# Attention units rebuilt around full 128 x 128 tiles, with masks added by TensorE, in a two-model fp32 layer kernel

## The reference, in short

```python
# FX (block one): 4 heads of 128
s = q @ k.T + (F_q - F_k);  s = where(k_pos <= q_pos, s, -inf);  p = softmax(s);  out = p @ v
# block two, 4 heads of 64, S = 512, per layer:
# MLA: heads of 96 = 64 + 32 rotary, values of 64, causal softmax
# NSA: o = g0 * attend(q, k_compressed (31 blocks)) + g1 * attend(q, selected) + g2 * attend(q, window)
#      (S = 512 makes selection and window causal over all keys; one key head for four query heads)
# DSA: score = sum_h w_h * relu(q_idx_h . k_idx), keep the top 128 keys of each query, softmax over them
# stick-breaking:
z = q @ k.T * scale;  mask = k_pos < q_pos
log_1m = where(mask, log_sigmoid(-z), 0);  after = cumsum(log_1m, reverse=True) - log_1m
a = where(mask, exp(log_sigmoid(z) + after), 0);  out = a @ v
```

## Time and profile before

| | |
|---|---|
| median of three runs | 3871.75 us |
| profiled execution, device time | 3873.97 us |
| its span, first to last instruction | 3872.2 us |
| mean granted TensorE clock | 0.898 |
| TensorE busy | 3588.0 us (93%) |
| VectorE, ScalarE, POOL busy | 1634.7, 1315.0, 335.9 us |

### The profile page before, as it was taken

How to read it: one execution, slowest core, us unless ns; L and a number is a source line. 1 busy time by engine, 2 the same in 40 slices (tenths; PEclk the granted TensorE clock), 3 DMA queues, 4 the chain that set the end, 5 groups by cost and what they waited for, 6 DMA issues and landing times. The chain is left out here.

```text
span 3872.2 us, 37493 instructions
## 1 busy us (share of the span) xinstructions
PE 3588.0 (93%) x14768; PEld 2731.7 (71%) x14768; DVE 1634.7 (42%) x2663; ACT 1315.0 (34%) x2225; POOL 335.9 (9%) x156
## 2 busy tenths in 40 slices
PE   6988889989999999898978999999998989699998
PEld 5755668878888888775545788878886655367886
DVE  3143431135343333356674533343344476654334
ACT  2324532233232222324354423232223243544222
POOL 0311324410000000130010000000002200100000
PEclk8988879999999999997556999999999965689999
DMA  3210213322333333320000233323332100012332
GB/s 125 77 38 26 77 40 97 98 82 95 96 98 98 98 95 97 101 71 28 1 1 22 87 96 95 98 87 94 96 98 95 55 17 1 0 55 87 96 96 76
DMA packets 76783, 279.82 MB, mean 72 GB/s; under 512 B 8768, under 2 KB 9024, under 8 KB 76224
## 3 DMA queue, kind: packets, MB, share of 16 engines
q1 hardware_dynamic: 76608, 277.42, 23.1%
HBM read 275.29 MB, written 2.10 MB: 72 GB/s over the span
## 5 line engine op out<-in xcount | busy, mean ns | idle before, releaser
L502 ACT ACTIVATE w_hi<-raw_slabs 128x1024 fp32r<-128x1024 f32 x496 | 524.3, 1058 | 1325.5 <-PE ps L542 1181.0
L517 DVE TENSOR_TENSOR w_lo<-raw_slabs,w_hi 128x1024 fp32r<-128x1024 f32 x376 | 459.9, 1224 | 740.3 <-ACT w_hi L502 740.1
L542 PE MATMUL ps<-in_hi,w_hi 128*128 128x512 f32 x1904 | 746.4, 392 | 9.9 <-DVE in_lo L816 9.9
L542 PE MATMUL ps<-in_hi,w_lo 128*128 128x512 f32 x1904 | 744.0, 391 | 0.0
L542 PE MATMUL ps<-in_lo,w_hi 128*128 128x512 f32 x1904 | 744.0, 391 | 0.0
L542 PE MATMUL ps<-parts,w_hi 128*128 128x512 f32 x2304 | 712.3, 390 | 7.7 <-PEq L378 7.7
L517 POOL TENSOR_TENSOR w_lo<-raw_slabs,w_hi 128x1024 fp32r<-128x1024 f32 x120 | 302.7, 2524 | 2429.9 <-ACT w_hi L502 2429.9
L542 PEld LDWEIGHTS ps<-parts,w_hi 128*128 128x128 f32 x2304 | 433.3, 188 | 100.0 <-issue 10.0
L542 PE MATMUL ps<-parts,w_lo 128*128 128x512 f32 x1152 | 448.9, 390 | 0.0
L542 PEld LDWEIGHTS ps<-in_hi,w_hi 128*128 128x128 f32 x1904 | 359.0, 189 | 91.3 <-DVE in_lo L816 8.9
L542 PEld LDWEIGHTS ps<-in_hi,w_lo 128*128 128x128 f32 x1904 | 359.4, 189 | 75.4
(11 more groups left out here) (258 smaller groups left out, 3640.9 us busy)
## 6 DMA issues: line engine op xcount, KB each, us to landing
raw_slabs<-weights SPq DMA_DIRECT2D x508, 512.0 KB, 3.6
big<-rope SPq DMA_DIRECT2D x2, 2304.0 KB, 10.1
x_resid<-xT SPq DMA_DIRECT2D x8, 256.0 KB, 4.5
outT<-x_resid SPq DMA_DIRECT2D x8, 256.0 KB, 2.0
const_cols<-consts SPq DMA_DIRECT2D x1, 1088.0 KB, 9.4
scratch<-brow SPq DMA_DIRECT2D x1, 768.0 KB, 10.6
vector_cols<-vec SPq DMA_DIRECT2D x2, 45.5 KB, 10.3
vector_cols<-vec SPq DMA_DIRECT2D x1, 69.0 KB, 3.0
```

The source lines that it names most:

```text
L502: self.nc.scalar.activation(self.w_hi[:, m % SPLIT, :], self.raw[:, n % RAW, :], ACT.Copy)\
L517: (self.nc.gpsimd if i is None else self.nc.vector).tensor_tensor(self.w_lo[:, m % SPLIT, :], self.raw[:, n % RAW, :], self.w_hi[:, m % SP ...
L542: mm = k.nc.tensor.matmul(out, lhsT, rhs, start=(c == 0 and m == 0), stop=(last and m == 2))
```

## The change

1. Scores and values use the whole array. In block two a head's query tile is used with all 128 rows; keys that two heads share are copied into an even and an odd tile, in which the other head's 64 rows are zero (`HalfKeys`, on POOL in the MLA up-projection and the index phase). Values are taken 128 columns wide (the neighbour's columns give rows of the result that are not stored).
2. The mask is one more matmul, identity times mask, into the score's bank: 128 columns for causal masks, 32 for the compressed unit, the whole width for DSA's selection. The compressed unit has a 32nd key, a floor, in place of the 0/1 multiply. Scales move to the query projections or into the exponential.
3. VectorE's maximum and ScalarE's exponential read PSUM; the score bank is free after the exponential.
4. Stick-breaking goes unit by unit, with one activation table; the exponent is completed in PSUM by a matmul; VectorE copies the transposed blocks.
5. `ahead` in `ResidNorm` goes by limits, after tiles 2, 4 and 6.

```diff
+def score(k, u, bank):
+    nc, w = k.nc, u.width
+    for j, (lhsT, rhs) in enumerate(u.scores):
+        nc.tensor.matmul(k.ps[:, bank, 0:w], lhsT, rhs, start=(j == 0), stop=False)
+    n = u.mask.shape[1]
+    return nc.tensor.matmul(k.ps[:, bank, w - n:w], k.c("ident"), u.mask, start=False, stop=True)
+def turn(k, u, p, bank):
+    for a, w in u.blocks:
+        mm = k.nc.tensor.transpose(k.ps[0:w, bank, a:a + P], p[:, a:a + w], k.c("ident"))
+    return mm
+def weigh(k, u, pt, bank):
+    for j, ((a, w), val) in enumerate(zip(u.blocks, u.values)):
+        mm = k.nc.tensor.matmul(k.ps[:, bank, 0:P], val, pt[0:w, a:a + P], start=(u.first and j == 0),
+                                stop=(u.last and j == len(u.blocks) - 1))
+    return mm
 ... # attention_phase, TensorE
-                        pe.wait_ge(masked, k.at(masked, i - 2))
-                    for j, (lhsT, rhs) in enumerate(u.scores):
-                        mm = nc.tensor.matmul(k.ps[:, i % 3, 0:u.width], lhsT, rhs, ...)
+                        pe.wait_ge(expd, k.at(expd, i - 2))
+                    score(k, units[i], i % 3).then_inc(scored, 1)
 ... # VectorE
-                    nc.vector.scalar_tensor_tensor(s, k.ps[:, i % 3, 0:u.width], u.scale, u.mask, ALU.mult, ALU.add)
-                    nc.vector.tensor_reduce(col(0, i), s, AX, ALU.max, negate=True).then_inc(row_max, 1)
+                    nc.vector.tensor_reduce(col(0, i), k.ps[:, i % 3, 0:u.width], AX, ALU.max, negate=True)
+                    if u.scale != 1.0:
+                        nc.vector.tensor_scalar(col(0, i), col(0, i), u.scale, None, ALU.mult)
 ... # ScalarE
-                    nc.scalar.activation(p, p, ACT.Exp, bias=col(0, i), accum_out=col(1, i)).then_inc(expd, 1)
+                    if i >= ring:
+                        act.wait_ge(turned, k.at(turned, i - ring + 1))
+                    nc.scalar.activation(probs(i)[:, 0:u.width], k.ps[:, i % 3, 0:u.width], ACT.Exp, bias=col(0, i),
+                                         scale=u.scale, accum_out=col(1, i)).then_inc(expd, 1)
 ... # stick_phase, TensorE, iteration i
+                    if i >= 4:
+                        pe.wait_ge(probs_ready, k.at(probs_ready, i - 3))
+                    score(k, units[i], i % 4).then_inc(scored, 1)
+                 # u = i - 2
+                    pe.wait_ge(rest, k.at(rest, u + 1))
+                    nc.tensor.matmul(bank(u), k.c("ident"), rest_at(u)[:, 0:units[u].width], start=False, stop=True, ...)
+                 # u = i - 3: turn, after probs_ready;  u = i - 4: weigh, after laid
 ... # ScalarE, iteration i: use_table(EXP_LN) once
+                    nc.scalar.activation(l, bank(i), ACT.Abs).then_inc(soft, 1)
+                    nc.scalar.activation(probs(u)[:, 0:units[u].width], bank(u), ACT.Exp).then_inc(probs_ready, 1)  # i - 2
+                    nc.scalar.activation(l, l, ACT.Exp, scale=-1.0).then_inc(soft, 1)
+                 # store of unit i - 5
+                    nc.scalar.activation(l, l, ACT.Ln, bias=1.0).then_inc(logged, 1)
 ... # VectorE, iteration i
+                 # u = i - 1: max(z, 0) + l from the bank, then the scan (multiplies by 1, subtracts l)
+                    take_top(k, dve, index, share(steps, i, n), steps.start)
+                 # u = i - 3
+                    nc.vector.tensor_copy(laid_at(u)[:, 0:cols], k.ps[:, turn_bank(u), 0:cols]).then_inc(laid, 1)
 ... # HalfKeys.gpsimd, per pair
+            nc.gpsimd.tensor_copy(odd[64:128], even[64:128]).then_inc(self.split, 1)
+            nc.gpsimd.memset(odd[0:64], 0.0).then_inc(self.halved, 1)
+            nc.gpsimd.memset(even[64:128], 0.0).then_inc(self.halved, 1)
 ... # ResidNorm.vector / .scalar
-                if n in (2, 5):
-                    ahead(1)
+                if n in (3, 5, 7):
+                    ahead(SLAB * (n // 2 - 1))
-            if n in (1, 4):
-                ahead(1)
-        ahead(NSLABS)
+            if n in (2, 4, 6):
+                ahead(SLAB * (n // 2 - 1))
+        ahead(NSLABS * SLAB)
 ... # token_phase, ScalarE
-            k.high_slabs(act, jobs[0][0])
-            norm.scalar(act, lambda most: k.high_slabs(act, jobs[0][0] + 4 * depth - 1, most))
+            norm.scalar(act, lambda i: k.high_slabs(act, jobs[0][0] + min(i, 4 * depth - 1)))
```

More of the change, by code:

```diff
@@ L1606, in attend @@
             pe.wait_ge(laid, k.at(laid, u - 1))
-        for a, w in units[u].blocks:
-            mm = nc.tensor.transpose(k.ps[0:w, 3 + u % 2, a:a + P], probs(u)[:, a:a + w], k.c("ident"))
-        mm.then_inc(turned, 1)
+        turn(k, units[u], probs(u), 3 + u % 2).then_inc(turned, 1)
     if 0 <= u - 2 < n:
@@ L1614, in attend @@
             pe.wait_ge(stored, k.at(stored, one.group - 2))
[L1615 to L1619, removed]
+        weigh(k, one, k.scr[:, 6 + (u - 2) % 3, :], 5 + one.group % 3).then_inc(unit_done, 1)
 def lay_and_store(k, act, u, n, units, turned, laid, unit_done, stored):
@@ L1651, in attention_phase @@
     gates = [sum(1 for u in units[:i + 1] if u.gate is not None) for i in range(n)]
+    scaled = [sum(1 for u in units[:i + 1] if u.scale != 1.0) for i in range(n)]
     groups = sum(1 for u in units if u.last)
@@ L1718, in stick_phase @@
                               "turned", "laid", "unit_done", "stored")]
-    n, batch = len(units), 4
-    ring = 3 * batch
-    batches = n // batch
-    rest_at = lambda i: k.scr[:, 10 + i % 2, :]
-    groups = sum(1 for u in units if u.last)
+    n = len(units)
+    bank = lambda i: k.ps[:, i % 4, 0:units[i].width]
+    turn_bank, out_bank = lambda i: 4 + i % 2, lambda i: 6 + i % 2
+    soft_at, rest_at, laid_at, probs = [lambda i, b=b: k.scr[:, b + i % 3, :] for b in (0, 3, 6, 9)]
+    assert all(u.first and u.last for u in units)
@@ L2220, in copy_in_phase, with softmax_units @@
     return here, 16 * len(later)
-def softmax_units(q, key, v, dims, width_of, masks, scale, group0, out, extra=None):
+def softmax_units(q, key, v, dims, masks, out, scale=1.0, extra=None):
     units = []
@@ L2229, in softmax_units @@
             lo = 64 * (h % 2) if dims == 64 else 0
-            units.append(Unit(pairs, w, [v(kb, h) for kb in range(qb + 1)], group0 + QB * h + qb, True, True,
-                              (lo, lo + dims), out(h)[lo:lo + dims, P * qb:P * qb + P], scale, mask=masks(qb)))
+            units.append(Unit(pairs, w, [v(kb, h) for kb in range(qb + 1)], QB * h + qb, True, True,
+                              (lo, lo + dims), out(h)[lo:lo + dims, P * qb:P * qb + P], masks(qb), scale))
     return units
@@ L2419, in layer @@
-    units = softmax_units(lambda h: half(tile(18 + h // 2), h), lambda h: half(tile(20), h),
-                          lambda kb, h: v_tok(kb)[:, VD0:VD0 + 64], 64, None,
-                          lambda qb: causal(0) if qb == 0 else select(qb)[:, 0:P * (qb + 1)], 64 ** -0.5, 0, ys(2))
+            qs = two_heads(14)(h)[:, P * qb:P * qb + P]
+            hidden = CONST.at["cmp_neg"][0] + wide * qb
+            units.append(Unit([(qs, kc[h % 2])], wide, [vc], first=True, last=False, gate=gate(0),
+                              mask=k.const[:, hidden:hidden + wide], **more))
@@ new lines, in layer @@
+            for b, (kt, col) in enumerate(((ks, VS0), (kw, VW0))):
+                units.append(Unit([(qs, one_half(kt)(h)[:, 0:wd])], wd, [shared(col)(kb, h) for kb in range(qb + 1)],
+                                  first=False, last=(b == 1), gate=gate(b + 1), mask=causal(qb), **more))
+    attention_phase(k, units, select, range(*TOP_CUTS))
+    units = softmax_units(two_heads(21), lambda h: tile(sk[h // 2][h % 2]),
+                          lambda kb, h: v_tok(kb)[:, VB0 + P * (h // 2):VB0 + P * (h // 2) + P], 64,
+                          lambda qb: k.c("strict"), ys(3))
```

296 lines of the change are left out of this document (159 added, 137 removed).

## The result

| | before | after |
|---|---|---|
| median of 4 runs, us | 3870.83 | 3650.83 (3650.66 to 3652.96) |
| ratio, 95% interval | | 0.943 (0.9412 to 0.9448) |
| span of the profiled execution, us | 3872.2 | 3649.1 |
| mean granted clock of TensorE | 0.898 | 0.959 |

A forecast was written before the change was run, and what follows sets the result against it. TensorE bounds the kernel, losing time to waits and low clock; gains 10 (MLA) + 101 (NSA) + 21 (DSA) + 19 (stick-breaking) + 17 (starts) - 3 (FX) - 1 (index) = 164 give 3708 us, range 3655 to 3775.

The forecast's parts named there:

- The mechanism: Attention stages: filled rows and columns, more than busy time, decide TensorE's clock; NSA gains 50 us a layer.
- A: Attention stages: the clock stays at 1.2 GHz although tiles are full, so filling is no lever; 3968 us, chance 0.03.
- B: Attention stages: the clock alternates as TensorE idles, a third of their time at the low clock; 3778 us, chance 0.12.
- C: Stick-breaking: its per-unit loop over three engines exceeds VectorE's 3.4 us per unit, stage stays at 73; 3739 us, chance 0.15.
- what would show it: NSA about 79 us, clock over 0.95, VectorE saturated; DSA 38 us, TensorE-bound; stick-breaking VectorE first; no 6 us start waits.
- the time put on top of the busiest engine: MLA, NSA, DSA: waits or fill and drain added to the busiest engine's time, 7 to 8, 9 and 5 us.
- The price of a full tile: Attention stages: a round of four units takes 6.1 us on TensorE at the full clock, 7.0 with causal masks.
- the scans of stick-breaking: Stick-breaking: scans stay on VectorE, priced at 51.4 us busy, needing 54; stage 63 us, gain 19 in two layers.
- The starts: Projections' starts: new slab points remove waits, 12 us in block one and 5 in two layers, 17 in all.
- Luck: FX: 16 added mask matmuls cost 5 us, less if the clock rises sooner; taken as 3 us slower.
- all lower ends together: Lower end of the range, 3655 us: every stage at its lower end and some 5 at the starts, 50 less.

The follow-up runs named there:

- masks_vector: The changed kernel, full tiles kept, with the mask added on VectorE from PSUM into SBUF in FX, MLA, NSA and DSA: 3693.4 us.

## Why the prediction came out as it did

- **The mechanism held.** Filled tiles raise the clock in NSA from 0.52 to 1.00, and half tiles take it away again for most of the stage. Rivals A and B did not come: the four stages show 0.91 to 1.00 over both layers, though NSA and MLA still leave TensorE gaps. Nor did C: stick-breaking gained almost twice its forecast. Of what would show it, two things did not come as written: DSA's 38 us, and a VectorE saturated through NSA. It is at 3.7 to 3.8 of 4 us in two thirds of the slices and at 64.70 of 75.90 overall; TensorE, 71.51, is first.
- **The first step that failed: the time put on top of the busiest engine.** The sum had 5 us of fill and drain in DSA, 9 us in NSA and 7 to 8 in MLA for engines that wait for each other. Measured are 0.2, 4.4 and 3.2. Over two layers that is about 27 of the 58 us by which the stages gained more than forecast. The allowance was read from MLA before, where VectorE was saturated and paced TensorE at a falling clock. With VectorE first again (masks_vector) MLA needs 6 us over its busiest engine, so it belonged to that state. The busiest engines themselves were priced well: TensorE 28 and VectorE 25.5 in MLA (28.9 and 25.4 measured), 70 and 66 in NSA (71.5 and 64.7).
- **The price of a full tile was a little too high.** I took 6.1 us for a round from a round of FX, by taking the four 4-row matmuls' own time off. But a 4-row matmul also makes its full neighbours longer: at the full clock FX's masks behind them take 326 ns and 274 with the padding. A DSA round with masks lasts 7.66 us (1951.83 to 1959.49), not 8.3. TensorE's 33 us there were 31.4, so of the 6.4 us that DSA's 38 missed, 1.6 are the tiles and 4.8 the fill and drain.
- **The second step that failed: the scans of stick-breaking.** VectorE was priced at 51.4 us, 54 with its pauses, and had 45.45. Of the 6 us 4.8 are the scans (13.2 in place of 18.0), since POOL's subtraction had delayed them; the prediction took the subtraction off POOL at no gain. That is 9.6 us in two layers. The 9 us of fill and drain were right: 54.3 - 45.45 = 8.9, with no pauses beside them.
- **The starts** took 15.2 us for the 12 forecast, the upper value that was given (15), and 8.5 for 5.
- **Luck.** FX came out 1 us better for a forecast 3 worse. By the estimate above its masks cost 4 us, and a low stretch of 20 us in place of 31 gave them back. mLSTM's 3.4 us are unchanged code as well. With FX's low stretch as long as before (5 us more) and mLSTM as before, the time would have been about 3659 us, an estimate, and inside the range. FX alone runs from 51.1 to 57.6 us in kernels with this same code, more than the 4 us by which the range was missed.
- **The range** took about 50 us off for all lower ends together, and they were nearly reached or passed in all stages at once. The allowances of NSA, MLA and DSA are one kind of error, so they should have been added in full, with more left below for the rest.

## What to carry to other kernels

Where TensorE is busy all the time at the lower granted clock, look at the shapes of its matmuls: try rows and columns padded to 128 with zeros, even in the one small matmul among large ones, before anything is moved between engines. Where a mask should be added is a question for each stage: on TensorE where VectorE is short (NSA), in place in PSUM by VectorE where TensorE is (DSA, FX). Price a tile from a stretch in which no other shape runs, and take off what POOL does to VectorE's scans before their duration is used for a version without POOL. Compare short stages only with the length of their low-clock stretch beside the time, since that moves with code elsewhere.

## What the runs showed of the hardware

- In NSA, with TensorE busy nearly throughout, the granted clock was 0.61 with half scores and half values, 0.86 with half scores, 1.00 with half values and 1.00 with full tiles. The 0.61 is 0.50 for over 100 us and then 1.00 on the same tiles, in both layers.
- A change between a partial and a full tile lengthens the full neighbour too: 593 to 644 ns at 512 columns. The half value matmul itself is no faster than the full one (282 against 276 ns), though its weight load is recorded as shorter (136 against 192 ns).
- With one 4-row matmul in each unit FX stood at a granted clock of 0.50 for 20 to 34 us, TensorE busy throughout; padded, for 3.4.
- A scan (1225 ns) started 0.02 us after a POOL subtraction of 1.26 us took 2.32 us. Started 0.05 us before one, the scans kept their time and POOL's took up to 1.70 us in place of 1.00. MAX8 and MATCH_REPLACE beside POOL took no longer than without.
- A VectorE addition in place in PSUM took 698 ns for 512 columns and 293 for 128, much as one from PSUM into SBUF (692 and 284).
